# Narrower waits for shift rows, gate loads and rotated sums, and the last head's norm moved behind a take

## The reference

```
h = rmsnorm(x, norm_w);  z = h @ w_in
# branch A, 8 heads: HGRN2 recurrence, then a norm by head and a gate
o_a = rmsnorm(hgrn2_chunked(q_a, 1 - f, log f, hi), hgrn_norm_w) * silu(hg)
y_a = o_a @ w_branch_a
# branch B, 8 heads of 64: three groups of dilated window attention
# (window, dilation) = (128,1), (512,4), (2048,16), RoPE on q and k
wts = exp(m_g - max_g m_g)
o_b = (sum wts*o_g) / (sum wts*l_g) * silu(ag);  y_b = o_b @ w_branch_b
merged = sigmoid(gates_a) * y_a + sigmoid(gates_b) * y_b
out = rmsnorm(x + merged @ w_out, final_norm_w)
```

## Time and profile before

| what | value |
|---|---|
| time, median of 3 runs | 1529.33 us (1528.75 to 1530.89) |
| the profiled execution | 1529.76 us |
| its span, first to last instruction | 1528.0 us |
| TensorE busy | 1495.0 us, 98% of the span |
| VectorE, ScalarE, GpSimd busy | 853.2, 704.9, 34.8 us |
| projections, L666 to L668 | 4176 matmuls, 1640 us of overlapping durations |
| mean granted clock of TensorE | 0.994 |

### The profile page before, as it was taken

One profiled execution on the slowest core, in us unless ns is written; L12 is line 12 of the kernel. 1 busy time (PEld: TensorE's weight loads), 2 busy tenths in 40 slices (PEclk: granted clock), 3 DMA queues, 4 the chain that ended last, 5 costly groups with the idle time before them and its releaser, 6 DMA issues. The chain is left out here.

```text
span 1528.0 us, 21088 instructions
## 1 busy us (share of the span) xinstructions
PE 1495.0 (98%) x7944; PEld 1279.6 (84%) x7944; DVE 853.2 (56%) x1384; ACT 704.9 (46%) x874; POOL 34.8 (2%) x39
## 2 busy tenths in 40 slices
PE   7999999999999999999999999999999998999998
PEld 6888888888888888887888878887888788788987
DVE  6646555564746464768942685268526854644523
ACT  6647566565656474736323524353335335311211
POOL 2000000000000000002200000000000000000000
PEclk9999999999999999999999999999999999999999
DMA  5111111121111112122303221322132214232602
GB/s 214 42 69 56 66 42 57 55 69 55 69 47 56 62 55 69 55 72 80 83 30 97 56 62 51 98 56 55 57 98 56 56 51 166 97 131 97 261 29 83
DMA packets 35376, 116.84 MB, mean 76 GB/s; under 512 B 6184, under 2 KB 6504, under 8 KB 35304
## 3 DMA queue, kind: packets, MB, share of 16 engines
q1 hardware_dynamic: 35312, 115.94, 22.9%
HBM read 83.21 MB, written 20.02 MB: 68 GB/s over the span
## 5 line engine op out<-in xcount | busy, mean ns | idle before, releaser
L666 PE MATMUL z_ps<-h_hi,w_hi 128*128 128x512 f32 x1392 | 552.0, 397 | 2.3 <-ACT zz L1145 2.3
L668 PE MATMUL z_ps<-h_hi,w_lo 128*128 128x512 f32 x1392 | 544.1, 391 | 0.0
L667 PE MATMUL z_ps<-h_lo,w_hi 128*128 128x512 f32 x1392 | 543.8, 391 | 0.0
L668 PEld LDWEIGHTS z_ps<-h_hi,w_lo 128*128 128x128 f32 x1392 | 262.0, 188 | 55.6
L666 PEld LDWEIGHTS z_ps<-h_hi,w_hi 128*128 128x128 f32 x1392 | 262.5, 189 | 54.2 <-issue 3.1
L667 PEld LDWEIGHTS z_ps<-h_lo,w_hi 128*128 128x128 f32 x1392 | 262.3, 188 | 50.5
L1280 DVE TENSOR_TENSOR w_lo<-w_stage,w_hi 128x1024 fp32r<-128x1024 f32 x89 | 109.4, 1229 | 224.5 <-ACT w_hi L992 224.2
L1000 ACT ACT_TABLE_LOAD x61 | 78.3, 1283 | 77.8 <-PE z_ps L668 77.1
L1092 ACT ACTIVATE pt<-pb 128x512 f32<-128x512 f32 (+1 forms) x80 | 43.5, 543 | 123.0 <-PE pb L810 122.6
L992 ACT ACTIVATE w_hi<-w_stage 128x1024 fp32r<-128x1024 f32 x89 | 93.8, 1054 | 0.4
L827 PE MATMUL pc<-pt,vb 128*128 128x128 f32 x560 | 77.7, 279 | 0.0
(11 more groups left out here) (247 smaller groups left out, 2210.3 us busy)
## 6 DMA issues: line engine op xcount, KB each, us to landing
w_stage<-w_in SPq DMA_DIRECT2D x88, 512.0 KB, 3.3
z_swap<-zz SPq DMA_DIRECT2D x96, 128.0 KB, 2.3
gate_d<-gate SPq DMA_DIRECT2D x16, 512.0 KB, 3.7
x_in<-x SPq DMA_DIRECT2D x8, 512.0 KB, 7.2
o_a_d<-o_a SPq DMA_DIRECT2D x8, 512.0 KB, 4.7
w_stage<-w_a SPq DMA_DIRECT2D x8, 512.0 KB, 3.3
cos_t<-gate_d SPq DMA_DIRECT2D x8, 512.0 KB, 3.3
sin_t<-gate_d SPq DMA_DIRECT2D x8, 512.0 KB, 4.3
```

What stands on the lines that cost most here:

```text
L666: nc.tensor.matmul(z_ps[hf][:], w_hi[s][:, k, :], h_hi[:, k, t], start=k == 0, stop=False)
L667: nc.tensor.matmul(z_ps[hf][:], w_hi[s][:, k, :], h_lo[:, k, t], start=False, stop=False)
L668: last = nc.tensor.matmul(z_ps[hf][:], w_lo[s][:, k, :], h_hi[:, k, t], start=False, stop=k == KT - 1)
```

## The change

SyncE waits before each group's pair of shift rows for that group's step of shift_done only, and each group has a semaphore of its own (rows_in[g]); TensorE waits for a group's rows at that group's first unit, and VectorE waits for those of groups 1 and 2 before its first sum, since the accumulators lie over m_rows. The load of gate tile 0 for j > 0 waits until both halves of the product that read the tile before are done, and no longer for the merged sum. GpSimd's wait for the transposes stands ahead of the level masks. VectorE's sums for group 2 move from slots 11 and 13 to slots 12 and 14, behind the maxima taken there and ahead of the weight split. ScalarE's norm factor for the eighth head moves within slot 4 of the first attention pass, from ahead of the q rounding to behind the take and the q copies.

```diff
--- before.py
+++ after.py
@@ -270,7 +270,8 @@
         rope_step, sin_done = sem("rope_step"), sem("sin_done")
         swapped, rope_a, rope_b, rope_sum = sem("swapped"), sem("rope_a"), sem("rope_b"), sem("rope_sum")
         qk_hi_done, qk_lo_done, q_dupped, k_copied = sem("qk_hi_done"), sem("qk_lo_done"), sem("q_dupped"), sem("k_copied")
-        padded, row_cleared, rows_in = sem("padded"), sem("row_cleared"), sem("rows_in")
+        padded, row_cleared = sem("padded"), sem("row_cleared")
+        rows_in = [sem(f"rows_in{g}") for g in range(GROUPS)]
         ag_stored, ag_loaded = sem("ag_stored"), sem("ag_loaded")
         avt_made, av_taken = sem("avt_made"), sem("av_taken")
         mx_made, mx_taken, mt_made, mt_taken = sem("mx_made"), sem("mx_taken"), sem("mt_made"), sem("mt_taken")
@@ -429,13 +430,13 @@
 
             def rows_to_queries(i):
 
-                shifted = value(sp, 3 * i + 3)
-                sp.wait_ge(const_in, 32)
-                sp.wait_ge(shift_done, shifted)
                 for g in range(GROUPS):
+                    shifted = value(sp, 3 * i + g + 1)
+                    sp.wait_ge(const_in, 32)
+                    sp.wait_ge(shift_done, shifted)
                     for h in range(2):
                         dst = q_sh[g][h][EDIM * (1 - h):EDIM * (1 - h) + 1, :]
-                        sp.dma_start(dst.bitcast(f32) if g < 2 else dst, m_rows[h:h + 1, g, :]).then_inc(rows_in, 16)
+                        sp.dma_start(dst.bitcast(f32) if g < 2 else dst, m_rows[h:h + 1, g, :]).then_inc(rows_in[g], 16)
 
             def attention(i, prev, cur):
                 for c in range(AT_CHUNKS):
@@ -530,7 +531,10 @@
                     load_stage(n + c + 2, c)
                     if j == c == 0:
                         sp.wait_ge(br_lo_done, N_BR - 1)
-                    if j:
+                    if j and c == 0:
+                        for s in range(2):
+                            sp.wait_ge(z_taken[s], n - 1)
+                    elif j:
                         sp.wait_ge(mg_sum, 2 * j)
                     sp.dma_start(g_in[c][:], gate_d[c, j]).then_inc(g_loaded[c], 16)
 
@@ -567,11 +571,11 @@
 
             pool.wait_ge(const_in, 32)
             pool.wait_ge(mask_loaded, 2 * 16)
+            pool.wait_ge(xt_made, 2 * KT)
             for m in range(6):
 
                 src = level_in[:, P * m:P * (m + 1)].rearrange("p (a c) -> p a c", a=1).to_broadcast([P, 4, P])
                 nc.gpsimd.tensor_copy(level_mask[:, m, :].rearrange("p (a c) -> p a c", c=P), src).then_inc(mask_done, 1)
-            pool.wait_ge(xt_made, 2 * KT)
             nc.gpsimd.memset(scores[:], 0.0).then_inc(mask_done, 1)
             nc.gpsimd.tensor_copy(mask_b[:], mask_in[:, 0:5, :].rearrange("p a b -> p (a b)")).then_inc(mask_done, 1)
             nc.gpsimd.tensor_copy(ident_b[:], ident[:]).then_inc(mask_done, 1)
@@ -787,8 +791,10 @@
                 g, h, m = UNITS[u]
                 base = (i - 1) * N_UNITS
                 if u == 0:
-                    pe.wait_ge(rows_in, i * 96)
+                    pe.wait_ge(shift_done, 3 * i)
                     pe.wait_ge(av_taken, i * 6)
+                if u in (0, 8, 16):
+                    pe.wait_ge(rows_in[g], i * 32)
                 if u >= 2:
                     pe.wait_ge(pt_done, base + u - 1)
                 pe.wait_ge(qk_lo_done, i * 4)
@@ -1099,7 +1105,8 @@
                         split_hi(n + 1, (c + 1) % 2)
                     if first(i):
 
-                        hgrn_tail(HEADS, slot)
+                        if slot != 4:
+                            hgrn_tail(HEADS, slot)
                         if slot == 0:
                             act.wait_ge(lvl_made, N_UNIT_HG * HEADS)
                         if slot == 5:
@@ -1173,6 +1180,8 @@
                                 if prev:
                                     act.wait_ge(den_ag, i)
                             take(n, hf, s_ag, ACT.Silu)
+                    if first(i) and slot == 4:
+                        hgrn_tail(HEADS, slot)
                     if first(i) and slot == 3:
                         act.wait_ge(rope_step, ROPE_STEPS)
                         nc.scalar.activation(cos_t[:], cos_t[:], ACT.Sin).then_inc(sin_done, 1)
@@ -1534,6 +1543,9 @@
                         for k in SUM_SLOTS.get(slot, ()):
                             g, h, b = k // 4, k // 2 % 2, k % 2
                             dve.wait_ge(pu_made, (i - 1) * N_UNITS + SUM_AFTER[k] + 1)
+                            if k == 0:
+                                for rows in rows_in[1:]:
+                                    dve.wait_ge(rows, i * 32)
                             if g == 0:
                                 nc.vector.tensor_copy(acc[h][:, HALF * b:HALF * (b + 1)], pc[:, b, :]).then_inc(ob_taken, 1)
                             else:
@@ -1545,6 +1557,18 @@
                         for g, m in MAX_SLOTS.get(slot - 1, ()):
                             for h in range(2):
                                 row_max(i, g, m, h)
+                    if cur and slot in (12, 14):
+
+                        j = (slot - 4) // 2
+                        dve.wait_ge(rope_a, i * 6 + j + 1)
+                        dve.wait_ge(rope_b, i * 6 + j + 1)
+                        if prev:
+                            dve.wait_ge(st_made, i * N_UNITS)
+                        for h in range(2):
+                            rows = slice(EDIM * h, EDIM * (h + 1))
+                            dst = (q_sh, k_sh)[j % 2][2][h]
+                            last = nc.vector.tensor_tensor(dst[rows, :], zz[j % 2][rows, :], z_swap[rows, :], ALU.add)
+                        last.then_inc(rope_sum, 1)
                     if cur and hf == 0:
                         split_lo(n + 1, (c + 1) % 2)
                     if first(i):
@@ -1581,15 +1605,7 @@
                         nc.vector.tensor_tensor(tokens(z_swap), tokens(z_swap), angle(sin_t), ALU.mult).then_inc(rope_b, 1)
                         dve.wait_ge(rope_a, i * 6 + j + 1)
                         dve.wait_ge(rope_b, i * 6 + j + 1)
-                        if j >= 4 and prev:
-                            dve.wait_ge(st_made, i * N_UNITS)
-                        if j >= 4:
-                            for h in range(2):
-                                rows = slice(EDIM * h, EDIM * (h + 1))
-                                dst = (q_sh, k_sh)[j % 2][2][h]
-                                last = nc.vector.tensor_tensor(dst[rows, :], zz[j % 2][rows, :], z_swap[rows, :], ALU.add)
-                            last.then_inc(rope_sum, 1)
-                        else:
+                        if j < 4:
                             nc.vector.tensor_tensor(zz[j % 2][:], zz[j % 2][:], z_swap[:], ALU.add).then_inc(rope_sum, 1)
                     if cur and 4 <= slot <= 10 and hf == 0:
                         j = (slot - 4) // 2
```

## The result

| | before | after |
|---|---|---|
| median | 1529.82 us, 4 runs (1528.75 to 1530.89) | 1520.61 us, 4 runs (1519.37 to 1521.6) |
| profiled execution, its span | 1529.76, 1528.0 us | 1521.0, 1518.9 us |
| mean granted clock of it | 0.994 | 0.998 |

The ratio is 0.9933, with a 95% interval of 0.9921 to 0.9945: 9.2 us less by the medians. The forecast was 10.1 us less, to 1519.5.

What follows compares the result with a forecast made beforehand. TensorE was taken to set the time, each standstill going straight to the end. 7.4 + 1.7 + 2.1 + 2.0 + 1.7 - 4.8 = 10.1 us less gave 1519.5 us, range 1516.5 to 1524.

Steps and rivals of the forecast that it cites:

- The norm: First attention pass: new stops of 3.0 and 3.8 us before slots 7 and 8, one clock fall; 4.8 us lost.
- The sums: Three passes: maxima ready 2.45 us sooner behind slot 12, 7.4 us gained, plus 1.7 for one clock fall gone.
- the cover called thin: Before slot 13's maxima: SyncE's later exchange still leaves about half a microsecond of margin, so it costs nothing.
- the rival of the late exchange: Three passes: exchange 1 us beyond the half microsecond in hand, costing three times 1 us, 1522 to 1526; chance 8%.
- the sign named for being wrong: Slot 8 of the first attention pass starting at 723 or sooner, or a new maxima stop one slot pair later.
- The shift rows: Last pass: 2.1 us gained in SyncE's queue; two stops of 1 to 2 us replace one of 4.
- The gate load: Second gate tile: the stop ending at 1331.91 goes, 2.0 us, and the clock fall behind it, 1.7 us.
- GpSimd: Start of the program: masks begin after the transposes, gaining between 0 and 0.3 us, taken as 0.
- The falls of the clock: TensorE's lower-clock stretches behind stops at 711, 905 and 1331 go, one comes near slots 7 and 8; 1.7 us each.

Runs made afterwards that it cites:

- the norm alone: The kernel before with nothing changed but ScalarE's norm for the eighth head moved behind the take and q copies: 1534.26 us, ratio 1.0029.
- The last kernel above: Changed kernel, norm later still, without VectorE's two self-waits, plus first two stored heads loaded before the last pass's shift rows: 1511.42 us, ratio 0.9873.

## Why the prediction held, point by point

**The norm: right, place and size.** Forecast 4.8 us lost, in two stops and one fall; measured 4.79 us. With the 0.42 us added back by which everything comes sooner from the start, each time of the chain is where it was put: rounding forecast 704.75, found 704.71; end of the norm 716.0 and 716.08; TensorE going on at 717.4 and 717.45; slot 8 at 726.75 and 726.74. The two stops were put at 3.0 and 3.8 us and are 2.64 and 3.56. The fall came behind the longer one only: clock 1.00 behind the 2.64 us, 0.52 behind the 3.56. That there would be one fall, and behind which stop, was a guess within the bounds of 3.1 and 6.5, and in part luck: in the norm alone it came behind the shorter stop, and the same move cost 3.2 us.

```profile
717.00:720.50 3.50, 3.47 (x15) 2.90 (x16) 3.49 (x3) 0.09 (x1) 1.97 (x3) 1.00 0.00 0
726.30:729.80 3.50, 3.48 (x9) 2.74 (x10) 3.50 (x2) 3.42 (x4) 0.00 (x0) 0.52 0.73 255
```

On ScalarE's table switches the trace speaks again: 710.73 to 715.66 us for both loads and three activations, 4.93 us in the new place. The drain that the Trainium skill (ScalarE: Activation LUTs, What ACT_TABLE_LOAD costs) gives each switch is not borne out here; with its figure, twice 1.38 us, slot 8 would by an estimate have started near 729.1 instead of 726.32.

**The sums: right in mechanism, 1.5 us too much.** Forecast 7.4 and a fall of 1.7, 9.1; the three passes gave 3.67 + 2.29 + 2.38, less 0.51 and 0.26 given back, so 7.6. The term failed in two ways. What stayed of the stops had been named but not taken off: behind slot 12 the passes gave 2.25, 2.29 and 2.38 us, not 2.45. And of the fall 1.4 came back, not 1.7. And the cover called thin, half a microsecond in front of slot 13's maxima, was not enough: the exchange was put at 903.58 + 2.4 us, with the 4.37 of the table 910.35, and was issued at 910.62; VectorE's rotation began 4.18 us after that, and its wait on itself, 0.34 us, was missing in the working. So TensorE lost 0.31 us at slot 14 of the second pass, 0.29 in the third and 0.04 in the fourth, and 0.2 more at the start of the third pass. That the wait decides is shown: without the waits of slots 11 and 13 nothing is lost at slot 14 any more, and 1.67 us come back in all. So the rival of the late exchange, given as 1 us in each pass, happened with a quarter of that. It is also the sign named for being wrong, a new stop for maxima one slot pair later, in gaps too short for the list of stops.

**The shift rows: right.** Forecast 2.1, measured 2.41 by the milestones, with the two stops as described. SyncE's queue, ScalarE and TensorE at the start of the last pass, against the earlier trace rows:

```profile
1254.22 3.70 SPq L439 DMA_DIRECT2D q_sh<-m_rows  x6
1257.97 0.57 SPq L526 DMA_DIRECT2D cos_t<-o_a_d  x1
```

The second row in the kernel before:

```profile
1263.50 0.58 SPq L525 DMA_DIRECT2D cos_t<-o_a_d  x1
```

```profile
1261.68 1.06 ACT L1222 ACTIVATE h_hi<-cos_t 128x1024 fp32r<-128x1024 f32 x1 [1.76 <-DMA cos_t<-o_a_d]
```

```profile
1259.98 1.16 PE L833 MATMUL pc<-pt,vb 128*128 128x128 f32 x8 [1.20 <-ACT pt L1098]
1263.27 1.16 PE L833 MATMUL pc<-pt,vb 128*128 128x128 f32 x8 [1.45 <-ACT pt L1098]
```

The first pair goes out with the copies, and the six still take 3.70 us. The last kernel above shows the second stop to be the stored head behind them in the queue, as the working said. What the working didn't see is that the old stop of 4.04 us had a fall of its own behind it (clock 0.55 above), while the two short ones have none.

**The gate load: right.** Forecast 3.7, measured 3.5 to the end, 3.6 alone. SyncE's queue, VectorE and TensorE, against the earlier trace rows:

```profile
1306.30 0.38 SPq L539 DMA_DIRECT2D cos_t<-gate_d  x1
```

```profile
1323.50 1.29 DVE L1666 TENSOR_TENSOR part<-z_ps,cos_t 128x512 f32<-128x512 f32 x2
```

```profile
1324.34 0.47 PE L898 MATMUL z_ps<-h_hi,w_hi 128*128 128x512 f32 x1
```

The load leaves 17 us before it is used, and neither engine stands.

**GpSimd: put at 0, 0.4 us in the profile.** Alone the ratio is 0.9994 with 1 in its interval, so it isn't told from nothing. The start also shifts, by -0.3 to +0.9 us, in kernels that leave GpSimd alone.

**The falls of the clock** were put by the place of each: three gone (at 711, 905 and 1331), one new. The profile lost four and got one: the fourth is that of the shift-row stop. It brought nothing beyond the 2.4 us there, since SyncE's queue and the stored head behind it end last: that load is issued 5.53 us sooner (rows above), of which 3.22 had been gained before. The experiments show that a place has no fixed fall, so to read the falls off one profile was a risk; single runs of the kernel before lie up to 3 us to either side of their middle. The total held because the profiled execution was near that middle, and because the changed kernel has few stops left that can be followed by a fall: its four runs all have a clock of 0.998. The 1 us by which the forecast was too high is the 1.5 of the sums less what the rows and the start gave beyond it.

## What to carry to other kernels

Before an engine's work is moved behind something, find what stands behind its consumer in the consumer's own list: here the norm's move freed 2 us in front of one slot and cost 6.2 in front of the next two, and VectorE's list said so. When a sum is moved out of a slot, move its waits with it; here a wait of VectorE on itself stood for a third of a microsecond each time, and the list of stops showed but a tenth of what those waits cost. Parts tried alone can each claim the same falls of the clock; compare the mean granted clock beside the time before adding gains, and read each part's gain at its own matmuls, against the same matmuls of the kernel before.

## What the runs showed of the hardware

**A fall is not fixed by its stop.** Stops of equal length after the same code had the clock at 0.52 behind them in one kernel and at 1.00 in another, and the kernel before ran with mean clocks from 0.992 to 0.996, over which its time goes from about 1534 to 1528 us.

**GpSimd and VectorE slow each other.** At the start, three normings of VectorE and six casts of GpSimd, first before, where they meet:

```profile
24.67 2.79 DVE L1298 TENSOR_SCALAR x_in<-x_in,x_rs 128x1024 f32<-128x1024 f32 x3
...
23.67 5.81 POOL L573 CAST level_mask<-gg 128x512 uint8<-128x512 f32 x6 [22.72 <-DMA vv<-c_mask]
...
36.98 0.17 DVE L1448 TENSOR_SCALAR lb<-lb 128x8 f32<-128x8 f32 x1
```

then after, where the casts start ten microseconds later:

```profile
24.36 2.08 DVE L1307 TENSOR_SCALAR x_in<-x_in,x_rs 128x1024 f32<-128x1024 f32 x3
...
34.31 3.40 POOL L578 CAST level_mask<-gg 128x512 uint8<-128x512 f32 x6 [33.36 <-PE pb L632]
...
37.22 1.42 DVE L1457 TENSOR_SCALAR lb<-lb 128x8 f32<-128x8 f32 x1
```

VectorE's three take 2.79 against 2.08 us and the casts 5.81 against 3.40. In the new place a VectorE operation on 8 columns takes 1.42 us beside GpSimd, where the one like it took 0.17 before. The kernel with GpSimd's wait alone shows that nothing else does it:

```profile
24.84 2.08 DVE L1298 TENSOR_SCALAR x_in<-x_in,x_rs 128x1024 f32<-128x1024 f32 x3
...
34.79 3.41 POOL L574 CAST level_mask<-gg 128x512 uint8<-128x512 f32 x6 [33.83 <-PE pb L628]
...
37.70 1.42 DVE L1448 TENSOR_SCALAR lb<-lb 128x8 f32<-128x8 f32 x1
```
